# Attention in groups of three quads, and the causal mask of the row maxima added on VectorE

## The chip, the cores and the metric

The kernel runs on one core of a Trainium2 chip. The metric is the device time of one execution in microseconds (us). The median of three runs of the kernel before is 3550.74 us (3547.54 to 3555.72).

## What is computed

One layer of a decoder with two branches, for a prompt of 4096 tokens and for 8 x 4 sampled tokens over a paged cache of 4096 positions. The change lies in the prompt's attention alone: 8 heads of width 64, 4096 queries and keys, float32:

```
s = einsum('bqhd,bkhd->bhqk', q, k) * ATTN_SCALE
s = s + (fq[..., :, None] - fk[..., None, :])      # sums of the log forget gates
s = where(k_pos <= q_pos, s, -inf)
p = softmax(s, axis=-1)
out = einsum('bhqk,bkhd->bqhd', p, v)
```

## The kernel before, in words

The program has five phases, one after another: `phase_project`, `phase_decode`, `phase_attend`, `phase_gates` and `phase_merge`. The change touches `phase_attend` only.

**Blocks and quads.** A block is one head and one tile of 512 queries; there are 64 (8 heads x 8 rows j = 0 to 7). The keys of a block come in quads of 512; row j has j + 1 quads, of which the last is on the diagonal. A head has 36 quads, the kernel 288. A quad is two steps; a step holds the scores of 256 keys by 512 queries, as two halves of 128 keys. `scores(s, half)` issues two matmuls (L1060, L1061) into the PSUM tile `st`, and for a diagonal quad a third, 128 columns wide, that adds the triangular mask (L1064). In diagonal quads the four halves have 512, 384, 256 and 128 columns. ScalarE takes the exponential of a step (L914, or four narrower ones a quad, L918) into `probs`, a ring of RING = 8 steps. GpSimd adds the four parts of a quad's probabilities (L880, L881), and one quad in two of a block to its neighbour (L865), in `quad_sum` with SUMS = 12 slots. `weigh(s)` multiplies the probabilities with v (L1081). `total(b)` takes the denominators of a block with ones (L1093), and `copy_den` on VectorE copies them out.

**Units.** The exponential needs a shift, the maximum of each row, before the block starts. So TensorE computes the scores a second time with queries on the partitions, in units: unit(b, t, c) is 128 queries by 512 keys, one matmul (L1031) into one of two PSUM banks `mx`, and VectorE takes the maximum of the unit (L971, TENSOR_REDUCE). There are 1152 units; 256 are diagonal (c = j), 64 each of 128, 256, 384 and 512 columns. For these TensorE adds the mask with a second matmul, identity by `tri`, 128 columns wide (L1034). The unit after next uses the same bank, and waits until VectorE has reduced it (`bank_free`). `combine(b)` (L978) takes the maximum over the parts of a block, `spread_shift(b)` (L1041, four matmuls) turns it, and ScalarE copies it into `q_one` (L896).

**Order.** TensorE's order is written out by a table. EARLY = 24 units come first, then 144 groups of two quads. A group is: the 8 halves of scores of its four steps, each followed by a unit where the table puts one; the shifts of the blocks that start in the next group (they wait for the exponential of all but the last step of the group, `exp_done`); the four steps of `weigh`; and the totals of blocks that ended one group earlier. A group has 9 units, or 7 if one of its quads is diagonal (after head 0); in a group of 7 no unit stands behind the last half of the diagonal quad. ScalarE waits, from the ninth step on, until the step eight earlier was weighed and its quad summed.

Of the kernel before, what the change touches and what calls it, by code (L numbers as in the profile page):

```python
# [617 lines left out]
def phase_attend(nc, io, keep):  # L618
# [6 lines left out]
    RING = 8  # L625
    SUMS = 12
# [6 lines left out]
    MASKS_READY = 17  # L633
# [15 lines left out]
    NGROUP = NQUAD // 2  # L649
    start_group = [quad_base[b] // 2 for b in range(NB)]  # L650
    end_group = [(quad_base[b + 1] - 1) // 2 for b in range(NB)]
# [10 lines left out]
    def most_units(g):  # L662
        return 7 if g >= quad_base[NT] // 2 and (on_diagonal(2 * g) or on_diagonal(2 * g + 1)) else 9
# [29 lines left out]
    def summed_with_next(n):  # L693

        c = n - quad_base[block_of[n]]
        return c % 2 == 0 and c < row(block_of[n])

# [14 lines left out]
    with ExitStack() as ctx:  # L712
# [7 lines left out]
        tri_raw = m.sb("tri_raw", [P, P])  # L720
        tri_t_raw = m.sb("tri_t_raw", [P, 2 * P])
        tri = m.sb("tri", [P, P], F32R)
# [6 lines left out]
        quad_sum = m.sb("quad_sum", [P, SUMS, TILE])  # L729
# [38 lines left out]
        def _(sp):  # L768
# [57 lines left out]
            for g in range(NGROUP):  # L826
# [7 lines left out]
                b = block_of[2 * g]  # L834
# [16 lines left out]
        def _(pool):  # L851
            nc.gpsimd.memset(tri_raw[:], 0.0)
            nc.gpsimd.memset(tri_t_raw[:], 0.0).then_inc(tri_ready, 1)
            pool.wait_ge(tri_ready, 1)
            nc.gpsimd.affine_select(out=tri_raw[:], in_=tri_raw[:], compare_op=ALU.is_ge, fill=-BIG, base=0,
# [5 lines left out]
            def end(n, last):  # L861

                if n > quad_base[block_of[n]] and summed_with_next(n - 1):
                    chain.link(last)
                    last = nc.gpsimd.tensor_tensor(quad_sum[:, n % SUMS], quad_sum[:, n % SUMS], quad_sum[:, (n - 1) % SUMS], ALU.add)  # L865
                last.then_inc(summed, 1)

            def add_quad(n):

                b = block_of[n]  # L870
                out = quad_sum[:, n % SUMS]
# [20 lines left out]
        def _(act):  # L892
# [42 lines left out]
        def _(dve):  # L935
# [22 lines left out]
            link(nc.vector.tensor_copy(tri[:], tri_raw[:]))  # L958
# [7 lines left out]
            def unit(k):  # L966
# [3 lines left out]
                dve.wait_ge(bank_ready, n + 1)  # L970
                nc.vector.tensor_reduce(max_parts[:, b % AHEAD, t, c:c + 1], mx[:, n % 2, 0:width], AX_X, ALU.max).then_inc(bank_done, 1)  # L971
# [37 lines left out]
        def _(pe):  # L1009
# [9 lines left out]
            def unit(k):  # L1019
                b, t, c = unit_at(k)  # L1020
                h, j = head(b), row(b)
                if k == unit_base[b]:
# [3 lines left out]
                    if j % 2 == 0:  # L1026
# [5 lines left out]
                                        k_one[h % 2][0:KM, c * TILE:c * TILE + width], start=True, stop=(c < j))  # L1032
# [1185 lines left out]
```

## Time and profile before

| | |
|---|---|
| median of three runs | 3550.74 us |
| the profiled execution | 3556.43 us, span 3554.8 us |
| PE busy (matmul) | 3303.2 us, 93% |
| DVE, POOL, ACT busy | 1627.9, 1338.1, 1126.3 us |
| mean granted TensorE clock | 0.96 of 2.4 GHz |

PE is TensorE's matmuls, PEld its weight loads, DVE VectorE, ACT ScalarE, POOL GpSimd. A busy time of PE is the sum of matmul durations, which overlap: the distance from one start to the next is what a matmul costs in the queue. "idle before" is the time in which the engine had nothing before an instruction, with the engine and line that ended it. phase_attend's units, scores and products lie between 1106 and 2545 us of the span.

### The profile page before, as it was taken

The page shows a single profiled execution, that of the slowest core. Times are in us where ns is not written, and L with a number is a line of the kernel's source. Part 1 is how long each engine was busy: PE and PEld are TensorE (multiplying, and loading weights), DVE is VectorE, ACT ScalarE, POOL GpSimd, SP SyncE. Part 2 cuts the span into 40 slices and gives each one's busy share as a digit, 9 for nine tenths or more (in the row PEclk, how much of TensorE's full clock was granted, in tenths as well). Part 3 has the DMA queues.
Part 4 walks back from the last instruction along what each step waited for, and adds up shares of the span by engine and source line. Part 5 has one row for each costly group of instructions (what it writes and reads, how often), then busy time and mean ns, then how long its engine had stood idle before and what let it go on. Part 6 is the DMA issues. An engine that isn't in the chain of part 4 may idle for free. (4 is left out here: it accounts for less than half of the span.)

```text
span 3554.8 us, 49146 instructions
## 1 busy us (share of the span) xinstructions
PE 3303.2 (93%) x17744; PEld 2365.7 (67%) x17744; DVE 1627.9 (46%) x2596; ACT 1126.3 (32%) x1532; POOL 1338.1 (38%) x1273
## 2 busy tenths in 40 slices
PE   8999999696964999999999999999799999959998
PEld 5777777572813666666666666666488888848876
DVE  3333332361615555555555555555343543445554
ACT  4222222141411444444444444454421121111111
POOL 0000000133331787788888888888600000000000
PEclk9999999797985999999999999999899999979999
DMA  5333443599987114141413131410311111055664
GB/s 182 132 125 128 142 158 113 173 365 366 367 312 143 44 37 87 36 89 35 86 37 85 37 85 37 85 33 11 112 72 47 47 68 74 24 183 182 206 206 155
DMA packets 239929, 435.41 MB, mean 122 GB/s; under 512 B 63544, under 2 KB 107577, under 8 KB 237664
## 3 DMA queue, kind: packets, MB, share of 16 engines
q1 hardware_dynamic: 216327, 362.34, 33.5%
q0 software_dynamic: 20768, 68.17, 5.1%
q10 hardware_dynamic: 2656, 2.62, 0.2%
q8 instruction: 101, 1.65, 0.2%
q14 instruction: 77, 0.62, 0.1%
HBM read 314.19 MB, written 119.03 MB: 122 GB/s over the span
## 5 line engine op out<-in xcount | busy, mean ns | idle before, releaser
L971 DVE TENSOR_REDUCE at_max_parts<-at_mx 128x1 f32<-128x512 f32 (+3 forms) x1152 | 737.0, 647 | 410.5 <-PE at_mx L1031 284.6
L914 ACT ACTIVATE at_probs<-at_st,at_gap 128x1024 f32<-128x1024 f32 x448 | 498.6, 1115 | 511.4 <-PE at_st L1061 511.1
L880 POOL TENSOR_TENSOR at_pair_sum<-at_probs 128x1024 f32<-128x1024 f32 x224 | 531.5, 2373 | 196.2 <-ACT at_probs L914 179.7
L1081 PE MATMUL at_o_ps<-at_probs,at_v 128*64 128x512 f32 (+3 forms) x2304 | 499.9, 566 | 0.0
L1031 PE MATMUL at_mx<-at_k_one,at_q_top 71*128 71x512 f32 (+3 forms) x1152 | 461.3, 402 | 14.0 <-DMA at_k_all<-scratch_k_parts 7.9
L1060 PE MATMUL at_st<-at_q_all,at_k_all 128*128 128x512 f32 (+3 forms) x1152 | 459.1, 399 | 6.9 <-ACT at_probs L918 5.6
L1061 PE MATMUL at_st<-at_q_one,at_k_one 67*128 67x512 f32 (+3 forms) x1152 | 440.1, 382 | 0.0
L1081 PEld LDWEIGHTS at_o_ps<-at_probs,at_v 128*64 128x64 f32 x2304 | 171.7, 137 | 246.4 <-issue 184.2
L93 PE MATMUL ga_acc<-ga_h_high,ga_w_high 128*128 128x512 f32 x768 | 299.8, 390 | 0.0
L95 PE MATMUL ga_acc<-ga_h_high,ga_w_low 128*128 128x512 f32 x768 | 299.6, 390 | 0.0
L94 PE MATMUL ga_acc<-ga_h_low,ga_w_high 128*128 128x512 f32 x768 | 299.6, 390 | 0.0
L881 POOL TENSOR_TENSOR at_quad_sum<-at_pair_sum 128x512 f32<-128x512 f32 x224 | 286.2, 1278 | 17.6
L1031 PEld LDWEIGHTS at_mx<-at_k_one,at_q_top 71*128 71x128 f32 x1152 | 221.2, 192 | 97.8 <-issue 41.7
L1060 PEld LDWEIGHTS at_st<-at_q_all,at_k_all 128*128 128x128 f32 x1152 | 220.1, 191 | 77.3 <-issue 43.0
L1061 PEld LDWEIGHTS at_st<-at_q_one,at_k_one 67*128 67x128 f32 x1152 | 220.5, 191 | 36.8
L1597 POOL MEMSET mg_minus_half<- 128x1 f32 x1 | 0.1, 98 | 583.9 <-POOLq L66 583.9
L93 PE MATMUL mg_acc<-mg_w_high,mg_mix_high 128*128 128x512 f32 x512 | 201.1, 393 | 5.2 <-DVE mg_x L1668 5.2
L93 PE MATMUL pj_acc<-pj_h_high,pj_w_high 128*128 128x512 f32 x512 | 202.9, 396 | 1.1 <-DVE pj_kv_rows L459 0.8
L95 PE MATMUL mg_acc<-mg_w_high,mg_mix_low 128*128 128x512 f32 x512 | 200.6, 392 | 0.0
L94 PE MATMUL mg_acc<-mg_w_low,mg_mix_high 128*128 128x512 f32 x512 | 200.3, 391 | 0.0
L296 POOL TENSOR_TENSOR pj_rms<-pj_squares,pj_eps_sum 128x1 f32<-128x1 f32 (+1 forms) x33 | 7.3, 221 | 511.2 <-ACT pj_junk L314 499.3
L95 PE MATMUL pj_acc<-pj_h_high,pj_w_low 128*128 128x512 f32 x512 | 199.6, 390 | 0.0
(318 smaller groups left out, 4957.7 us busy)
## 6 DMA issues: line engine op xcount, KB each, us to landing
dc_pages<-in_cache_k_dram SPq DMA_DIRECT2D x128, 256.0 KB, 5.3
dc_pages<-in_cache_k_dram POOLq DMA_DIRECT2D x128, 256.0 KB, 5.3
dc_pages<-in_cache_v_dram SPq DMA_DIRECT2D x128, 256.0 KB, 8.1
dc_pages<-in_cache_v_dram POOLq DMA_DIRECT2D x128, 256.0 KB, 5.4
scratch_h_t<-pj_h_t SPq DMA_DIRECT2D x8, 2048.0 KB
scratch_q_parts<-pj_stage SPq DMA_DIRECT2D x32, 512.0 KB, 3.4
scratch_k_parts<-pj_stage SPq DMA_DIRECT2D x32, 512.0 KB, 2.8
at_q_all<-scratch_q_parts SPq DMA_DIRECT2D x128, 128.0 KB
```

The costliest lines, as they stand in the source:

```text
L93: nc.tensor.matmul(out, lhs_high, rhs_high, start=first, stop=False)
L94: nc.tensor.matmul(out, lhs_high, rhs_low, start=False, stop=False)
L95: return nc.tensor.matmul(out, lhs_low, rhs_high, start=False, stop=last)
L296: chain.link(nc.gpsimd.tensor_tensor(out, squares[0:rows, n:n + 1], eps_sum[0:rows], ALU.add))
L880: chain.link(nc.gpsimd.tensor_tensor(pair, first, second, ALU.add))
L881: end(n, nc.gpsimd.tensor_tensor(out, pair[:, 0], pair[:, 1], ALU.add))
L914: nc.scalar.activation(probs[:, s % RING], st[:, s % 2], ACT.Exp, bias=bias).then_inc(exp_done, 1)
L971: nc.vector.tensor_reduce(max_parts[:, b % AHEAD, t, c:c + 1], mx[:, n % 2, 0:width], AX_X, ALU.max).then_inc(bank_done, 1)
L1031: last = nc.tensor.matmul(mx[:, n % 2, 0:width], q_top[0:KM, b % AHEAD, t * P:(t + 1) * P], k_one[h % 2][0:KM, c * TILE:c * TILE + width], ...
L1060: nc.tensor.matmul(out, k_all[h % 2][:, keys], q_all[:, b % AHEAD, at:TILE], start=True, stop=False)
L1061: last = nc.tensor.matmul(out, k_one[h % 2][0:KR, keys], q_one[0:KR, b % AHEAD, at:TILE], start=False, stop=(c < j))
L1081: last = nc.tensor.matmul(o_ps[half * HD:(half + 1) * HD, b % 2, at:TILE], v[:, h % 2, 4 * c + own], probs[:, s % RING, half, at:TILE], st ...
```

## The change

- A group has three quads (QUADS = 3, STEPS = 6): 96 groups instead of 144, with 12 halves of scores and then six steps of `weigh`. The ring of probabilities has 12 steps. A group has at most 13 units, or 12 with a diagonal quad after head 0, spread over the twelve places behind the halves; with 12 or fewer none is at the group's start, and with 12 there is one behind the last half of a diagonal quad too. EARLY becomes 29.
- `quad_sum` has 6 slots for the quads that go to `total`, and one for the quads that are added to their neighbour.
- The mask matmul L1034 is gone. For the 256 diagonal units VectorE issues `tensor_tensor_reduce` instead of `tensor_reduce`: it adds `tri` (now float32, 512 wide, zero but for the last 128 columns) to the unit in its PSUM bank, in place, and takes the maximum. It is built as two instructions, both ISA below: the operation, and a second one that writes the 128x1 result and signals.

```diff
-    RING = 8
-    SUMS = 12
+    QUADS = 3
+    STEPS = 2 * QUADS
+    RING = 2 * STEPS
+    SUMS = 6
...
     def most_units(g):
-        return 7 if g >= quad_base[NT] // 2 and (on_diagonal(2 * g) or on_diagonal(2 * g + 1)) else 9
+        return 4 * QUADS if g >= quad_base[NT] // QUADS and any(on_diagonal(QUADS * g + i) for i in range(QUADS)) else 4 * QUADS + 1
...
-        if len(units) > 8:
+        if len(units) > 2 * STEPS:
             return units[place:place + 1]
-        skipped = 8 - len(units)
-        at_end = 4 if on_diagonal(2 * g) else 8
-        places = [p for p in range(1, 9) if p != at_end][:len(units)] if skipped == 1 else list(range(1, 1 + len(units)))
+        places = [1 + i * 2 * STEPS // len(units) for i in range(len(units))]
...
+    def sum_slot(n):
+
+        return SUMS if summed_with_next(n) else kept.index(n) % SUMS
...
@@ GpSimd @@
-                if n >= SUMS:
-                    pool.wait_ge(bank_ready, bank_of["den", block_of[n - SUMS]] + 1)
+                if not summed_with_next(n) and kept.index(n) >= SUMS:
+                    pool.wait_ge(bank_ready, bank_of["den", block_of[kept[kept.index(n) - SUMS]]] + 1)
...
@@ VectorE, unit(k) @@
+                if c == row(b):
+                    nc.vector.tensor_tensor_reduce(out=mx[:, n % 2, 0:width], in0=mx[:, n % 2, 0:width], in1=tri[:, TILE - width:TILE], scale=1.0,
+                                                   scalar=NO_MAX, op0=ALU.add, op1=ALU.max,
+                                                   accum_out=max_parts[:, b % AHEAD, t, c:c + 1]).then_inc(bank_done, 1)
+                    return
                 nc.vector.tensor_reduce(max_parts[:, b % AHEAD, t, c:c + 1], mx[:, n % 2, 0:width], AX_X, ALU.max).then_inc(bank_done, 1)
...
@@ TensorE, unit(k) @@
-                                        k_one[h % 2][0:KM, c * TILE:c * TILE + width], start=True, stop=(c < j))
-                if c == j:
-                    last = nc.tensor.matmul(mx[:, n % 2, t * P:width], ident_r[:], tri[:], start=False, stop=True)
+                                        k_one[h % 2][0:KM, c * TILE:c * TILE + width], start=True, stop=True)
...
@@ TensorE, the groups @@
-                for place in range(8):
-                    scores(4 * g + place // 2, place % 2)
+                for place in range(2 * STEPS):
+                    scores(STEPS * g + place // 2, place % 2)
                     for k in units_after(g, place + 1):
                         unit(k)
                 if starting(g + 1):
-                    pe.wait_ge(exp_done, 4 * g + 3)
+                    pe.wait_ge(exp_done, STEPS * g + STEPS - 1)
                 for b in starting(g + 1):
                     spread_shift(b, starting(g + 1)[0])
-                for s in range(4 * g, 4 * g + 4):
+                for s in range(STEPS * g, STEPS * g + STEPS):
                     weigh(s)
```

TensorE in head 1, row 6, before: the end of a group with a diagonal unit of 256 columns (L1031 and its mask L1034 are the unit, L1060 and L1061 scores, L1081 the product with v, L1093 the total).

```order
L1031 MATMUL at_mx<-at_k_one,at_q_top 128x256
L1034 MATMUL at_mx<-at_tri,at_ident_r 128x128
L1060 MATMUL at_st<-at_q_all,at_k_all 128x512
L1061 MATMUL at_st<-at_q_one,at_k_one 128x512
L1031 MATMUL at_mx<-at_k_one,at_q_top 128x512
L1081 MATMUL at_o_ps<-at_probs,at_v 64x512 x8
L1093 MATMUL at_mx<-at_quad_sum,keep_ones 32x128 x12
```

The same engine in head 1, row 7, in the changed kernel, the end of a group with a diagonal unit of 384 columns (the lines are now L1041 for the unit, L1068, L1069, L1089 and L1101).

```order
L1041 MATMUL at_mx<-at_k_one,at_q_top 128x384
L1068 MATMUL at_st<-at_q_all,at_k_all 128x512
L1069 MATMUL at_st<-at_q_one,at_k_one 128x512
L1041 MATMUL at_mx<-at_k_one,at_q_top 128x512
L1089 MATMUL at_o_ps<-at_probs,at_v 64x512 x12
L1101 MATMUL at_mx<-at_quad_sum,keep_ones 32x128 x16
```

The mask matmul is gone, and twelve products stand together where eight stood. The last places of a group that ends with a diagonal quad, before:

```order
L1031 MATMUL at_mx<-at_k_one,at_q_top 128x384
L1034 MATMUL at_mx<-at_tri,at_ident_r 128x128
L1060 MATMUL at_st<-at_q_all,at_k_all 128x128
L1061 MATMUL at_st<-at_q_one,at_k_one 128x128
L1064 MATMUL at_st<-at_tri_t,at_ident_r 128x128
L1041 MATMUL at_st<-at_ident_r,at_shift_w 65x128 x4
```

And in the changed kernel (L1072 is the mask of the scores, L1049 the shift):

```order
L1041 MATMUL at_mx<-at_k_one,at_q_top 128x512
L1068 MATMUL at_st<-at_q_all,at_k_all 128x128
L1069 MATMUL at_st<-at_q_one,at_k_one 128x128
L1072 MATMUL at_st<-at_tri_t,at_ident_r 128x128
L1041 MATMUL at_mx<-at_k_one,at_q_top 128x512
L1049 MATMUL at_st<-at_ident_r,at_shift_w 65x128 x4
```

A unit now stands between the last half of scores and the shift. VectorE in head 0 of the changed kernel. Before, only `L971 TENSOR_REDUCE` stood here, one a unit, between the small ones that combine and copy:

```order
L977 ISA at_max_parts 128x1
L981 TENSOR_REDUCE at_max_parts<-at_mx 128x1 x2
L977 ISA at_mx,at_max_parts<-at_mx,at_tri 128x256
L977 ISA at_max_parts 128x1
L981 TENSOR_REDUCE at_max_parts<-at_mx 128x1 x2
L977 ISA at_mx,at_max_parts<-at_mx,at_tri 128x384
```

Each diagonal unit is two instructions on VectorE where it was one.

## Rows read from the trace of the kernel before

**Rows 1.** Busy us in a stretch: PE, PEld, DVE, ACT, POOL; clock; DMA share, GB/s.

```profile
1440.00:2500.00 1060.00, 1053.28 (x5878) 681.27 (x5876) 574.28 (x965) 524.99 (x628) 855.51 (x627) 1.00 0.25 54
```

**Rows 2.** Timeline of PE: start us, duration us, instruction; a unit with its mask.

```profile
1519.52 0.40 PE L1031 MATMUL at_mx<-at_k_one,at_q_top 71*128 71x512 f32 x1
1519.76 0.23 PE L1034 MATMUL at_mx<-at_tri,at_ident_r 128*128 128x128 f32 x1
1519.82 0.47 PE L1060 MATMUL at_st<-at_q_all,at_k_all 128*128 128x512 f32 x1
1520.13 0.41 PE L1061 MATMUL at_st<-at_q_one,at_k_one 67*128 67x512 f32 x1
1520.37 0.40 PE L1031 MATMUL at_mx<-at_k_one,at_q_top 71*128 71x512 f32 x1
1520.60 0.40 PE L1060 MATMUL at_st<-at_q_all,at_k_all 128*128 128x512 f32 x1
```

**Rows 3.** Timeline of PE over the end of a group and the next one's start.

```profile
2354.49 0.39 PE L1031 MATMUL at_mx<-at_k_one,at_q_top 71*128 71x512 f32 x1
2354.81 3.65 PE L1081 MATMUL at_o_ps<-at_probs,at_v 128*64 128x512 f32 x16
2358.39 0.50 PE L1060 MATMUL at_st<-at_q_all,at_k_all 128*128 128x512 f32 x1
2358.73 0.39 PE L1061 MATMUL at_st<-at_q_one,at_k_one 67*128 67x512 f32 x1
2358.96 0.22 PE L1031 MATMUL at_mx<-at_k_one,at_q_top 71*128 71x128 f32 x1
...
2359.42 0.40 PE L1061 MATMUL at_st<-at_q_one,at_k_one 67*128 67x512 f32 x1
```

**Rows 4.** Timeline of PE: a diagonal quad at a group's end.

```profile
1511.22 0.22 PE L1064 MATMUL at_st<-at_tri_t,at_ident_r 128*128 128x128 f32 x1
1511.28 0.45 PE L1031 MATMUL at_mx<-at_k_one,at_q_top 71*128 71x512 f32 x1
1511.57 0.28 PE L1060 MATMUL at_st<-at_q_all,at_k_all 128*128 128x256 f32 x1
...
1512.38 0.28 PE L1064 MATMUL at_st<-at_tri_t,at_ident_r 128*128 128x128 f32 x1
1512.70 0.45 PE L1041 MATMUL at_st<-at_ident_r,at_shift_w 128*65 128x128 f32 x4
1513.08 3.22 PE L1081 MATMUL at_o_ps<-at_probs,at_v 128*64 128x512 f32 x16
1516.23 0.43 PE L1093 MATMUL at_mx<-at_quad_sum,keep_ones 128*32 128x128 f32 x8
```

**Rows 5.** Groups by line and shape, DVE: count, busy us, mean ns, idle before.

```profile
L971 DVE TENSOR_REDUCE at_max_parts<-at_mx 128x1 f32<-128x512 f32 x960 | 659.9, 691 | 306.0 <-PE at_mx L1031 284.6 <-PE at_mx L1034 3.1
L971 DVE TENSOR_REDUCE at_max_parts<-at_mx 128x1 f32<-128x128 f32 x64 | 18.6, 290 | 42.7 <-PE at_mx L1034 42.6
L1394 DVE TENSOR_TENSOR ga_stage<-ga_acc,ga_stage 128x512 f32<-128x512 f32 x32 | 22.1, 692 | 155.5 <-ACT ga_stage L1303 150.8 <-DVE ga_pooled L1387 4.3
```

**Rows 6.** Timeline of DVE, a small operation between two others.

```profile
2323.97 0.19 DVE L978 TENSOR_REDUCE at_shift_w<-at_max_parts 128x4 fp32r<-128x32 f32 x1
2324.08 0.28 DVE L971 TENSOR_REDUCE at_max_parts<-at_mx 128x1 f32<-128x128 f32 x1
```

**Rows 7.** Groups by line, ACT: the accumulator read of the projection's squares.

```profile
L314 ACT ACTIVATION_READ_ACCUMULATOR pj_junk<-pj_x 128x1 f32 x28 | 5.2, 187 | 0.0
```

**Rows 8.** Groups by line and shape, POOL.

```profile
L880 POOL TENSOR_TENSOR at_pair_sum<-at_probs 128x1024 f32<-128x1024 f32 x224 | 531.5, 2373 | 196.2 <-ACT at_probs L914 179.7 <-POOL at_quad_sum L865 8.3 <-POOL at_quad_sum L881 7.8
L881 POOL TENSOR_TENSOR at_quad_sum<-at_pair_sum 128x512 f32<-128x512 f32 x224 | 286.2, 1278 | 17.6
```

**Rows 9.** Timeline of DVE among the units ahead of the first group.

```profile
1111.00 1.02 DVE L971 TENSOR_REDUCE at_max_parts<-at_mx 128x1 f32<-128x512 f32 x2 [0.68 <-PE at_mx L1031]
1112.58 1.15 DVE L971 TENSOR_REDUCE at_max_parts<-at_mx 128x1 f32<-128x512 f32 x2 [0.55 <-PE at_mx L1031]
```

More of the change, by code:

```diff
@@ L647, in phase_attend @@
     unit_base = [TT * quad_base[b] for b in range(NB + 1)]
-    NGROUP = NQUAD // 2
-    start_group = [quad_base[b] // 2 for b in range(NB)]
-    end_group = [(quad_base[b + 1] - 1) // 2 for b in range(NB)]
+    NGROUP = NQUAD // QUADS
+    start_group = [quad_base[b] // QUADS for b in range(NB)]
+    end_group = [(quad_base[b + 1] - 1) // QUADS for b in range(NB)]
     def on_diagonal(n):
@@ L696, in summed_with_next @@
         return c % 2 == 0 and c < row(block_of[n])
+    kept = [n for n in range(NQUAD) if not summed_with_next(n)]
+    def sum_slot(n):
+        return SUMS if summed_with_next(n) else kept.index(n) % SUMS
     def dens_after(g):
@@ L719, in phase_attend @@
         q_one = m.sb("q_one", [P, AHEAD, TILE], F32R)
-        tri_raw = m.sb("tri_raw", [P, P])
+        tri = m.sb("tri", [P, TILE])
         tri_t_raw = m.sb("tri_t_raw", [P, 2 * P])
-        tri = m.sb("tri", [P, P], F32R)
         tri_t = m.sb("tri_t", [P, 2 * P], F32R)
@@ L728, in phase_attend @@
         pair_sum = m.sb("pair_sum", [P, 2, TILE])
-        quad_sum = m.sb("quad_sum", [P, SUMS, TILE])
+        quad_sum = m.sb("quad_sum", [P, SUMS + 1, TILE])
         den_out = m.sb("den_out", [P, 2, P])
@@ L851, in _ @@
         def _(pool):
-            nc.gpsimd.memset(tri_raw[:], 0.0)
+            nc.gpsimd.memset(tri[:], 0.0)
             nc.gpsimd.memset(tri_t_raw[:], 0.0).then_inc(tri_ready, 1)
             pool.wait_ge(tri_ready, 1)
-            nc.gpsimd.affine_select(out=tri_raw[:], in_=tri_raw[:], compare_op=ALU.is_ge, fill=-BIG, base=0,
+            nc.gpsimd.affine_select(out=tri[:, TILE - P:TILE], in_=tri[:, TILE - P:TILE], compare_op=ALU.is_ge, fill=-BIG, base=0,
                                     pattern=[[-1, P]], channel_multiplier=1).then_inc(tri_ready, 1)
@@ L864, in end @@
                     chain.link(last)
-                    last = nc.gpsimd.tensor_tensor(quad_sum[:, n % SUMS], quad_sum[:, n % SUMS], quad_sum[:, (n - 1) % SUMS], ALU.add)
+                    last = nc.gpsimd.tensor_tensor(quad_sum[:, sum_slot(n)], quad_sum[:, sum_slot(n)], quad_sum[:, SUMS], ALU.add)
                 last.then_inc(summed, 1)
@@ L870, in add_quad @@
                 b = block_of[n]
-                out = quad_sum[:, n % SUMS]
+                out = quad_sum[:, sum_slot(n)]
                 first, second = probs[:, 2 * n % RING], probs[:, (2 * n + 1) % RING]
                 pool.wait_ge(exp_done, 2 * n + 2)
-                if n >= SUMS:
-                    pool.wait_ge(bank_ready, bank_of["den", block_of[n - SUMS]] + 1)
+                if not summed_with_next(n) and kept.index(n) >= SUMS:
+                    pool.wait_ge(bank_ready, bank_of["den", block_of[kept[kept.index(n) - SUMS]]] + 1)
                 if n + 1 < quad_base[b + 1]:
@@ L1048, in scores @@
                 if half == 0:
-                    if s % 4 == 0 and starting(s // 4):
-                        pe.wait_ge(shift_copied, starting(s // 4)[-1] + 1)
+                    if s % STEPS == 0 and starting(s // STEPS):
+                        pe.wait_ge(shift_copied, starting(s // STEPS)[-1] + 1)
                     if s == first_step[b]:
@@ L1092, in total @@
                     for t in range(TT):
-                        last = nc.tensor.matmul(mx[t * 32:(t + 1) * 32, n % 2, 0:P], keep["ones"][:, 0:32], quad_sum[:, q % SUMS, t * P:(t + 1) * P],
+                        last = nc.tensor.matmul(mx[t * 32:(t + 1) * 32, n % 2, 0:P], keep["ones"][:, 0:32], quad_sum[:, sum_slot(q), t * P:(t + 1) * P],
                                                 start=(q == quads[0]), stop=(q == quads[-1]))
@@ L1108, in _ @@
                 if starting(g + 1):
-                    pe.wait_ge(exp_done, 4 * g + 3)
+                    pe.wait_ge(exp_done, STEPS * g + STEPS - 1)
                 for b in starting(g + 1):
                     spread_shift(b, starting(g + 1)[0])
-                for s in range(4 * g, 4 * g + 4):
+                for s in range(STEPS * g, STEPS * g + STEPS):
                     weigh(s)
```

6 lines of the change are left out of this document (3 added, 3 removed).

## The prediction

> **What bounds the kernel now.** I read four views in this order. First the stretches: in 1060 us in the middle of the attention PE is busy for 1053 us at full clock, while DVE has 574 us, ACT 525 us and POOL 855 us [rows 1]. PE is the limit there, so a change pays only by what it takes out of PE's queue, or costs by what makes PE wait. Second, the timeline of PE, for what an instruction costs in that queue. With 512 columns the start-to-start distance is 0.235 us for scores and units alike: 1520.13 to 1520.60 are two slots [rows 2]. A half of scores with its unit is thus three slots, 0.705 us. Third, the groups of DVE: a unit of 512 columns takes 0.691 us [rows 5], just under PE's 0.705. DVE is idle 306 us before them all the same, since no units come while PE multiplies with v. Fourth, POOL's groups: a full quad costs 2.37 + 1.28 us, and every second one 1.28 us more for the addition to its neighbour, 4.3 us on average [rows 8]. PE needs 4 x 0.705 = 2.82 us for the scores and units of a full quad and 1.72 us for its product (below), 4.54 us. POOL is second.
>
> **1. The mask matmul goes (256 times).** From a masked unit to the second scores matmul behind it is 1519.52 to 1520.13, 0.61 us; without the mask these are two slots, 0.47 us. That is 0.14 us here [rows 2]. For narrow units I have a pair without a mask: a matmul of 128 columns followed by a 512 one, then the next: 1511.22, 1511.28, 1511.57, that is 0.06 + 0.29 = 0.35 us [rows 4]. A masked unit of 128 columns takes 2358.96 to 2359.42 = 0.46 us to the same point [rows 3]. That is 0.11 us, and I take this for all widths: of the two places read it is the lower. A small matmul is too short to cover the next weight load, so the price is twice the 0.06 us that its own columns take. 256 x 0.11 = 28.2 us; in the opening stretch (24 units, 9 of them masked) DVE sets the pace and nothing is won: **-27 us**. Bounds: 256 x 0.06 = 15 us and 256 x 0.14 = 36 us.
>
> The Trainium skill, TensorE: Matmul & The Clock Gate, section "Wait — 56ns, not 53.3ns?", gives a warm 128-column matmul 56 ns from start to start. By that figure alone the term would be an estimated 14 us; rows 2 and 3 both show about double, so the measurement decides.
>
> **2. 96 changes of kind instead of 144.** From the last unit of a group to the first product is 0.32 us instead of 0.235: 0.085 more. Eight products take 3.58 us (the row's 16 are two records each) [rows 3]. A group with a diagonal quad needs 1513.08 to 1516.23 = 3.15 us [rows 4]. Products go in pairs side by side, so that group has 256 columns less, 0.43 us; 512 columns are 0.86 us, four pairs 3.44, and 0.14 us of the 3.58 is paid once a group. The first scores behind it take 0.34 us to the next instead of 0.235, 0.10 more [rows 3]. Together 0.325 us a group; 48 fewer: **-15.6 us**. Bounds: 48 x 0.2 and 48 x 0.33.
>
> **3. Places of the units.** Behind a diagonal quad at the end of a group PE stands from 1512.38 to 1512.70, 0.32 us for a slot of 0.06, until ScalarE has done the last but one step [rows 4]. The change puts a unit there, and also behind a diagonal quad at a group's start, where scores wait for ScalarE. By the table 40 and 24 of the 64 diagonal quads lie so. A slot of up to 0.235 us is then covered by a wait; but in a diagonal quad PE's places are 0.5 to 0.7 us apart and DVE needs 0.69, so most of it goes to waiting for the bank. I take 0.06 each: **-4 us**, between -15 (all of it) and +10 (DVE late by 0.15 us in each).
>
> **4. Opening.** Five more units stand ahead of the first group, where two units take 1.58 us [rows 9]: 5 x 0.79 = 4.0 us, less 5 x 0.235 later, **+2.7 us**. The wider memset of `tri` on POOL is hidden by the load of the keys.
>
> **5. The new instruction on DVE.** Not in the trace. Lower bound: it costs what the reduction does, as adding a PSUM tile and an SBUF tile of 512 columns takes 0.692 us [rows 5]. The second instruction: a small operation of DVE delays the next by 0.11 us [rows 6]; ScalarE's accumulator read is 0.187 us long [rows 7]. I take e = 0.10 us over the reduction, nearest to DVE's own row. What covers it: twelve units of 0.691 are 8.29 us; 2.67 of twelve are diagonal and on average 0.20 us shorter (0.290 at 128 columns, 0.691 at 512 [rows 5]), -0.53; so DVE needs 7.76 + 2.67e = 8.03 us a group. PE wants the bank for the twelfth unit 11 x 0.705 + 0.47 = 8.2 us after the group's start, and needs the tenth reduced by then. DVE starts at 0.9 and has ten at 0.9 + 8.03 x 10/12 = 7.6. There are 0.6 us to spare, 0.3 in a group with a diagonal quad. **0 us**, for any e up to 0.19. Below nothing it cannot be, since PE, busy for 1053 of 1060 us, waits for DVE almost nowhere now [rows 1].
>
> **6. POOL, SP, end.** POOL's 4.3 us plus gaps of about 0.1 us between operations stay under PE's 4.54, and the ring still holds two groups. The slots of `quad_sum` are never needed in the group in which their total is still due (worked through by the table). In the last head the units run out and ScalarE and POOL set the pace for nine quads: **+1 us** of part 2 not won. SP's loads of q still come five groups or more ahead of their units.
>
> **Sum.** -27 - 15.6 - 4 + 2.7 + 1 = -43 us against the profiled execution's 3556.4 us, so 3513. That execution is 5.7 us above the median; against the median the forecast is **3507 us**. Its own range is 3495 to 3522, from the bounds of parts 1 to 3 without all ends meeting.
>
> **Rivals.**
> - *Half rate.* With two float32 tensors DVE takes two cycles a column. The slope of rows 5 is 0.401 us over 384 columns, 1.04 ns a column; 320 columns on average are 0.33 us more, e = 0.43. Ten units are done at 0.9 + 8.91 x 10/12 = 8.3 us: 0.1 us late in 90 groups and 0.3 more in the 56 with a diagonal quad, 25 us: **3532 us**. Against it: the addition at 0.692 us [rows 5]. Chance 0.12. The Trainium skill, Vector Engine (DVE) Microarchitecture Reference, in its list of pitfalls, says that this kind of instruction runs at half throughput with two non-bf16 sources in SBUF; here one source is in PSUM, and no row shows the case.
> - *DVE becomes the bound (slower).* The instruction makes two full passes: 0.49 us more (the mean of the four widths by rows 5) and a read of 0.187, e = 0.68. Ten units at 0.9 + 9.58 x 10/12 = 8.9 us, 0.7 late in 90 groups, +61 us: **3568 us**. It decides from e = 0.58 on, where the lateness, (7.76 + 2.67e) x 10/12 + 0.9 - 8.2, equals the 0.45 us a group that parts 1 to 4 bring. For it: DVE has only 2% to spare against PE's places already. Chance 0.07.
> - *POOL takes over.* Its operations in full quads, gaps included, may reach 4.6 us; then PE's gain in rows 4 to 7 of a head turns into waits of ScalarE for the ring, and only part 1 in the small rows and some of part 2 stay, 25 us: **3526 us**. Against: POOL has 855 of 1060 us [rows 1]. Chance 0.08.
> - *Nothing is won.* The small matmul's slot and the pause at a group's end were only cover for DVE, and PE stands for the bank instead: parts 1 to 3 fall away, **3550 us**. Against: in rows 2 DVE is never what PE waits for. Chance 0.06.
>
> **Numbers.** Forecast 0.67. The range of 3488 to 3542 us takes in the forecast's own, half rate and POOL, reaches 7 us below the forecast's own for part 3 at its best, and leaves out the other two. A measurement of this kernel can tell about 0.2%, 7 us. Faster by more: 0.67 + 0.12 + 0.08 = 0.87, less something for a price that no row shows: 0.85. Same 0.07, slower 0.08.
>
> **What would show it.** The masked stretch must read 0.47 us from unit to second scores. Twelve products must take 3 x 1.72 + 0.14 = 5.3 us. The stretch from the first unit to the last total, 1106 to 2545 us now, must shrink by the whole sum, and the rest of the span by nothing. The new instruction's pair should occupy DVE for 0.8 us at 512 columns, and idle time of PE ended by it should stay under 15 us. A pair of 1.2 us or more with PE idle behind it is half rate; POOL at over 90% of the middle stretch is the third rival. I am wrong above all if the diagonal units cost DVE more than 0.4 us extra.

## The result and the profile after

| | before | changed |
|---|---|---|
| median of four runs each, one chip | 3553.23 us | 3521.20 us |
| lowest to highest | 3547.54 to 3557.71 | 3513.22 to 3525.18 |
| ratio, with its 95% interval | | 0.9908 (0.9884 to 0.9931) |

By the ratio that is 33 us faster, 25 to 41 by the interval. The forecast was 43 us faster against the profiled execution; between the two profiled spans it is 3554.8 - 3519.9 = 34.9 us. The sign and the mechanisms came out as forecast, and the gain is four fifths of the sum.

The head of the changed kernel's page, and the stretch that answers to [rows 1] (busy us of PE, PEld, DVE, ACT and POOL with the number of instructions, then the granted clock, the DMA share and GB/s):

```profile
span 3519.9 us, 48877 instructions
PE 3266.0 (93%) x17488; PEld 2339.1 (66%) x17488; DVE 1632.7 (46%) x2851; ACT 1124.0 (32%) x1532; POOL 1335.7 (38%) x1273
```

```profile
1440.00:2500.00 1060.00, 1054.06 (x5848) 676.91 (x5845) 574.92 (x1149) 538.83 (x647) 885.91 (x647) 1.00 0.24 55
```

PE is as full as before, 1054 of 1060 us, at full clock: what left its queue became time. POOL went from 855 to 886 us because the same work is now done in less time; at 84% it is not the limit.

VectorE's groups by shape, those of [rows 5] and the new instruction (line, engine, operation, shapes and count; busy us and mean ns; idle before):

```profile
L981 DVE TENSOR_REDUCE at_max_parts<-at_mx 128x1 f32<-128x512 f32 x896 | 612.6, 690 | 180.4 <-PE at_mx L1041 166.1
L977 DVE CUSTOM_DVE_ANT_0 at_mx<-at_mx,at_tri 128x512 f32<-128x512 f32 x64 | 44.8, 700 | 32.9 <-PE at_mx L1041 31.9
L977 DVE DVE_READ_ACCUMULATOR2_ANT at_max_parts<- 128x1 f32 x256 | 36.1, 141 | 0.0
L977 DVE CUSTOM_DVE_ANT_0 at_mx<-at_mx,at_tri 128x128 f32<-128x128 f32 x64 | 18.6, 291 | 12.2 <-PE at_mx L1041 12.2
```

The masked maximum has the pace of the reduction, 700 against 690 ns at 512 columns. The second instruction, which reads the accumulator, is 141 ns long. Whether it delays the next unit is read from DVE's timeline in one group (start and length in us), with the unit of TensorE that the last line waits for:

```profile
1527.30 3.39 DVE L981 TENSOR_REDUCE at_max_parts<-at_mx 128x1 f32<-128x512 f32 x5 [0.21 <-PE at_mx L1041]
1530.64 0.57 DVE L977 CUSTOM_DVE_ANT_0 at_mx<-at_mx,at_tri 128x384 f32<-128x384 f32 x1
1531.12 0.14 DVE L977 DVE_READ_ACCUMULATOR2_ANT at_max_parts<- 128x1 f32 x1
1531.35 3.51 DVE L981 TENSOR_REDUCE at_max_parts<-at_mx 128x1 f32<-128x512 f32 x5
...
1530.91 0.40 PE L1041 MATMUL at_mx<-at_k_one,at_q_top 71*128 71x512 f32 x1
```

From the masked unit of 384 columns to the next is 0.71 us, but that is not what the instruction costs: the next unit's matmul runs until 1530.91 + 0.40 = 1531.31, and the reduction starts 0.04 us behind it. In this stretch DVE follows PE's pace. DVE's own pace shows only where the next unit stands ready, and the third experiment has such places: there a masked unit delays the next operation by no more than a plain reduction does. What remains of the second instruction is that it ends later. At 384 columns it ends at 1531.12 + 0.14 = 1531.26, 0.62 us behind the start, where a plain reduction is 0.557 us long (by its group in the third experiment); the bank is given back 0.07 us later.

TensorE at the end of a group with a diagonal quad, which answers to [rows 4]:

```profile
1544.49 0.22 PE L1041 MATMUL at_mx<-at_k_one,at_q_top 71*128 71x128 f32 x1
1544.55 0.45 PE L1068 MATMUL at_st<-at_q_all,at_k_all 128*128 128x512 f32 x1
1544.84 0.39 PE L1069 MATMUL at_st<-at_q_one,at_k_one 67*128 67x512 f32 x1
...
1546.41 0.45 PE L1041 MATMUL at_mx<-at_k_one,at_q_top 71*128 71x512 f32 x1
1546.87 0.28 PE L1072 MATMUL at_st<-at_tri_t,at_ident_r 128*128 128x128 f32 x1
1547.06 0.50 PE L1041 MATMUL at_mx<-at_k_one,at_q_top 71*128 71x512 f32 x1
1547.40 0.41 PE L1049 MATMUL at_st<-at_ident_r,at_shift_w 128*65 128x128 f32 x4
1547.73 4.94 PE L1089 MATMUL at_o_ps<-at_probs,at_v 128*64 128x512 f32 x24
1552.60 0.64 PE L1101 MATMUL at_mx<-at_quad_sum,keep_ones 128*32 128x128 f32 x16
```

The narrow unit without its mask stands 0.35 us ahead of the second scores matmul, as forecast. The last place of the group now has a unit: from the mask of the scores, 1546.87, it is 0.19 us to the unit (the bank) and 0.34 to the shift. The 0.53 us hold a unit where 0.32 us held nothing. The twelve products with a diagonal quad among them take 4.87 us; twelve full ones 5.30 by the same view, as forecast.

### The profile page after: what moved, and what is told of

It is laid out like the page before. It is cut to its first block and busy times, and to the rows that moved or that the text cites. A ratio compares the mean times of both kernels' runs of the same rounds, so it can differ in the third digit from the quotient of the medians.

```text
span 3519.9 us, 48877 instructions
## 1 busy us (share of the span) xinstructions
PE 3266.0 (93%) x17488; PEld 2339.1 (66%) x17488; DVE 1632.7 (46%) x2851; ACT 1124.0 (32%) x1532; POOL 1335.7 (38%) x1273
## 5 line engine op out<-in xcount | busy, mean ns | idle before, releaser
L981 DVE TENSOR_REDUCE at_max_parts<-at_mx 128x1 f32<-128x512 f32 x896 | 612.6, 690 | 180.4 <-PE at_mx L1041 166.1
L1089 PE MATMUL at_o_ps<-at_probs,at_v 128*64 128x512 f32 (+3 forms) x2304 | 490.2, 564 | 0.0
L1041 PE MATMUL at_mx<-at_k_one,at_q_top 71*128 71x512 f32 (+3 forms) x1152 | 466.6, 407 | 18.0 <-DMA at_k_all<-scratch_k_parts 7.8
L1068 PE MATMUL at_st<-at_q_all,at_k_all 128*128 128x512 f32 (+3 forms) x1152 | 449.3, 390 | 4.3 <-ACT at_probs L920 1.6
L1069 PE MATMUL at_st<-at_q_one,at_k_one 67*128 67x512 f32 (+3 forms) x1152 | 440.8, 383 | 0.0
L1089 PEld LDWEIGHTS at_o_ps<-at_probs,at_v 128*64 128x64 f32 x2304 | 179.5, 137 | 261.3 <-issue 219.4
L1041 PEld LDWEIGHTS at_mx<-at_k_one,at_q_top 71*128 71x128 f32 x1152 | 221.4, 192 | 109.5 <-DVE at_max_parts L981 23.6
L1068 PEld LDWEIGHTS at_st<-at_q_all,at_k_all 128*128 128x128 f32 x1152 | 220.4, 191 | 66.5 <-issue 27.4
L1069 PEld LDWEIGHTS at_st<-at_q_one,at_k_one 67*128 67x128 f32 x1152 | 220.7, 192 | 37.1
```

Source lines behind the costliest of these rows:

```text
L1041: last = nc.tensor.matmul(mx[:, n % 2, 0:width], q_top[0:KM, b % AHEAD, t * P:(t + 1) * P], k_one[h % 2][0:KM, c * TILE:c * TILE + width], ...
L1068: nc.tensor.matmul(out, k_all[h % 2][:, keys], q_all[:, b % AHEAD, at:TILE], start=True, stop=False)
L1069: last = nc.tensor.matmul(out, k_one[h % 2][0:KR, keys], q_one[0:KR, b % AHEAD, at:TILE], start=False, stop=(c < j))
L1089: last = nc.tensor.matmul(o_ps[half * HD:(half + 1) * HD, b % 2, at:TILE], v[:, h % 2, 4 * c + own], probs[:, s % RING, half, at:TILE], st ...
```

## The experiments

Each was timed beside the kernel before on its own chip; the medians of that kernel beside them lie between 3553.23 and 3558.24 us, so the ratios and the traces are what can be compared. "Attention" is the time from the start of the first unit to the start of the last matmul of the last total, in the profiled execution; "head" is the distance between the same totals of two heads in the middle of it; "first product" is where `weigh` first issues, counted from the first unit.

| run | median us | ratio (95%) | attention | head | first product |
|---|---|---|---|---|---|
| before | | 1 | 1438.4 | 176.1 | +34.4 |
| changed | 3521.20 | 0.9908 (0.9884 to 0.9931) | 1402.5 | 170.3 | +43.4 |
| groups only | 3540.20 | 0.9956 (0.9942 to 0.9969) | 1420.9 | 172.9 | +43.7 |
| mask only | 3534.63 | 0.9943 (0.9929 to 0.9956) | 1416.8 | 173.1 | +34.1 |
| DVE work twice | 3564.24 | 1.0019 (1.0010 to 1.0028) | 1445.7 | 176.2 | +44.3 |
| small matmuls in the opening | 3517.17 | 0.9888 (0.9873 to 0.9903) | 1397.1 | 170.4 | +38.4 |
| changed, again | 3518.30 | 0.9902 (0.9889 to 0.9915) | 1401.4 | 170.3 | +43.0 |
| small matmuls, again | 3513.38 | 0.9883 (0.9868 to 0.9898) | 1395.7 | 170.4 | +38.7 |
| places from 0 | 3521.69 | 0.9907 (0.9894 to 0.9920) | 1405.0 | 171.0 | +43.1 |
| mask twice (before) | 3579.10 | 1.0072 (1.0057 to 1.0087) | 1462.1 | 179.0 | +36.3 |
| two quads, ring 12 | 3535.97 | 0.9935 (0.9923 to 0.9948) | 1416.2 | 172.8 | +34.4 |
| three quads, ring 8 | 3518.18 | 0.9885 (0.9870 to 0.9899) | 1404.0 | 170.3 | +45.1 |
| small matmuls, v later | 3508.21 | 0.9858 (0.9844 to 0.9873) | 1389.2 | 170.5 | +31.6 |

**One part alone.** The changed kernel with the mask matmul back, and the kernel before with the mask on VectorE. Of each edit the central lines are shown; the making of `tri`, and the lines that the shown ones replace, are left out.

```diff
 TensorE, unit(k), changed kernel
+                if c == j:
+                    last = nc.tensor.matmul(mx[:, n % 2, t * P:width], ident_r[:], tri[:], start=False, stop=True)
```

> Groups of three, the mask still added by TensorE (L1034's matmul kept, VectorE reduces as before). Theory (the parts add up: mask -27, groups and places about -17 us before the opening's cost): 13 to 20 us faster than the kernel before. A middle head (176.1 us before, 170.3 after) at about 173.8. Rival 1 (the mask's slot is only cover for VectorE and all of the gain is the groups'): 30 us faster, the same as the change. Rival 2 (larger groups bring nothing): no change.

```diff
 kernel before: VectorE, unit(k)
+                if c == row(b):
+                    nc.vector.tensor_tensor_reduce(out=mx[:, n % 2, 0:width], in0=mx[:, n % 2, 0:width], in1=tri[:, TILE - width:TILE], scale=1.0,
+                                                   scalar=NO_MAX, op0=ALU.add, op1=ALU.max,
+                                                   accum_out=max_parts[:, b % AHEAD, t, c:c + 1]).then_inc(bank_done, 1)
+                    return
```

> Groups of two as before, mask added by VectorE. Theory: 256 x 0.11 = 27 us faster less what VectorE's second instruction makes PE wait, 20 to 27 us; a middle head at about 172.6. Rival 1 (the slot was cover): PE waits for the bank instead, less than 7 us faster, with PE idle behind the new instruction. If e1 and e2 add up to more than the change's own 32 to 36 us, the parts stand in each other's way.

The groups alone bring 16 us by the ratio (17.5 of attention), the mask alone 20 (21.6). Their sum, 39 us in the traces, is near the 36 of both together. Per head the groups save 3.2 us and the mask 3.0; together 5.8. The forecast, without its opening and end, was 46.6 / 8 = 5.8 us a head. But eight heads at 3.2 us would be 26 us for the groups, and the trace has 17.5. The rest is lost outside the middle heads: the first product stands at +43.7 instead of +34.4.

The parts do stand in each other's way a little: 3.2 + 3.0 a head is 0.4 us more than 5.8, so behind the groups the mask brings 172.9 - 170.3 = 2.6. PE's idle time ahead of the units that DVE's maxima end is 8.4 us in all before, 10.2 with the groups alone, 22.5 with the mask alone and 30.7 in the changed kernel. Most of it comes with the mask on VectorE; the groups alone add next to none.

**How near DVE is to being the bound.** One more reduction of the same bank ahead of each masked one, its result unused.

```diff
+                    nc.vector.tensor_reduce(spare[:, b * TT + t:b * TT + t + 1], mx[:, n % 2, 0:width], AX_X, ALU.max)
                     nc.vector.tensor_tensor_reduce(
```

> The changed kernel with one more reduction of the same unit ahead of each diagonal unit's instruction, so the diagonal unit costs VectorE 0.49 us more on average (0.29 to 0.69), e = about 0.6 in all. My sum gave a break-even at e = 0.58: the time should come back to that of the kernel before, within 10 us. Rival (the two banks and the products absorb more than I counted): under 15 us slower than the changed kernel. Other rival (VectorE already sets the pace): the full 256 x 0.49 = 125 us slower than the changed kernel.

DVE in this kernel where both units stand ready (L978 is the spare reduction, L979 the masked maximum and its read), the middle stretch, and PE's idle time ahead of all units that L979 ends:

```profile
1803.73 0.56 DVE L978 TENSOR_REDUCE at_spare<-at_mx 128x1 f32<-128x384 f32 x1 [5.74 <-PE at_mx L1043]
1804.21 0.56 DVE L979 CUSTOM_DVE_ANT_0 at_mx<-at_mx,at_tri 128x384 f32<-128x384 f32 x1
1804.68 0.14 DVE L979 DVE_READ_ACCUMULATOR2_ANT at_max_parts<- 128x1 f32 x1
1804.68 0.69 DVE L978 TENSOR_REDUCE at_spare<-at_mx 128x1 f32<-128x512 f32 x1
1805.28 0.69 DVE L979 CUSTOM_DVE_ANT_0 at_mx<-at_mx,at_tri 128x512 f32<-128x512 f32 x1
1805.89 0.14 DVE L979 DVE_READ_ACCUMULATOR2_ANT at_max_parts<- 128x1 f32 x1
1805.89 0.69 DVE L983 TENSOR_REDUCE at_max_parts<-at_mx 128x1 f32<-128x512 f32 x1
```

```profile
1440.00:2500.00 1060.00, 1043.03 (x5681) 655.78 (x5679) 640.54 (x1349) 523.20 (x628) 854.88 (x627) 1.00 0.24 54
...
  DVE at_max_parts L979: 88.1, 208
```

The distance from one start to the next is 0.47 or 0.48 us at 384 columns and 0.60 or 0.61 at 512, whether the operation is the plain reduction or the masked one, and the read starts together with the next operation. So at these widths the price of the masked maximum in DVE's queue is e = 0.0, and the spare reduction adds 0.61, 0.48, 0.33 and 0.20 us at 512, 384, 256 and 128 columns, 0.41 on average.

The whole gain is gone and 7 us more: the changed kernel's attention grows by 43 us. The crossing lies below 0.41, where the prediction put it at 0.58. Its own sum gave the half-rate rival, at e = 0.43, only 25 us. PE's busy time falls from 1054 to 1043 of 1060 us, though DVE is busy for only 641: PE stands ahead of a unit for 88.1 / 208 = 0.42 us at a time until a masked unit's bank is free, 208 times for 256 of them. Not all of these 88 us are lost, but the lateness is paid at each masked unit and does not average over ten. That the time came back near that of the kernel before, as expected, is partly luck: the added work was smaller than reckoned, and the cover was thinner.

**The opening.** Two small full-float32 matmuls behind each of the 29 first units, into a part of `st` that is written later anyway.

```diff
             for k in range(EARLY):
                 unit(k)
+                for i in range(2):
+                    nc.tensor.matmul(st[:, 1, 1, 0:P], keep["ones"][:], keep["ident"][:], start=True, stop=True)
```

> The changed kernel with two more matmuls of 128 columns in full float32 (ones by identity, result unused) behind each of the 29 opening units, where TensorE stands idle between units. It tests whether the clock, 0.50 until about 48 us after the first unit in the changed kernel and until about 37 us in the kernel before, is what the opening loses. Theory: PE busy in the opening brings the clock to 1.00 before the first group, and the first group runs in half the time: 6 to 12 us faster than the changed kernel. Rival (the clock rises only with the products and the extra work just delays the units): no change or up to 10 us slower.

The ratio, 0.9888, lies inside the interval of the changed kernel's first comparison, so both were run again, side by side.

> The changed kernel itself, unaltered, as the yardstick for the three runs beside it on the same chip. Both theories: 32 to 36 us faster than the kernel before.

> The kernel of e4 once more, now beside e5. In e4's trace the units ran from 1106.3 to 2451.5 us, 7 us less than in the changed kernel. Theory (the clock in the opening is worth what that trace shows): 5 to 9 us faster than e5. Rival (the gain is noise of other phases): within 3 us of e5.

Side by side it is 3518.30 against 3513.38, 4.9 us, just under the expected 5 to 9, and 5.7 us of attention. The two intervals, 0.9889 to 0.9915 and 0.9868 to 0.9898, overlap, so the traces carry this verdict. Stretches of 10 us (busy us of PE, PEld, DVE, ACT and POOL; the number behind POOL is the clock), first of the changed kernel:

```profile
1124.00:1134.00 10.00, 9.32 (x23) 5.09 (x23) 6.59 (x15) 1.07 (x2) 0.00 (x0) 0.50 1.10 216
1134.00:1144.00 10.00, 10.00 (x29) 8.26 (x29) 5.32 (x11) 4.22 (x6) 3.22 (x5) 0.50 1.15 213
1144.00:1154.00 10.00, 10.00 (x39) 6.43 (x39) 2.86 (x6) 3.08 (x6) 6.54 (x7) 0.58 0.96 212
1154.00:1164.00 10.00, 10.00 (x52) 7.69 (x52) 8.04 (x16) 7.43 (x10) 5.17 (x3) 1.00 0.47 122
```

With the small matmuls, second run (this execution began the attention 1.1 us earlier). The first three stretches are cut where the clock changed:

```profile
1103.22:1109.50 6.28, 6.28 (x27) 6.09 (x28) 3.08 (x10) 0.00 (x0) 0.00 (x0) 0.50 1.32 225
1109.50:1116.30 6.80, 4.52 (x35) 4.17 (x34) 4.29 (x12) 0.00 (x0) 0.00 (x0) 1.00 1.05 221
1116.30:1123.20 6.90, 6.11 (x24) 5.73 (x25) 2.80 (x6) 0.00 (x0) 0.00 (x0) 0.51 1.05 220
1123.00:1133.00 10.00, 9.31 (x74) 8.65 (x73) 8.82 (x19) 1.07 (x2) 0.00 (x0) 0.99 1.10 213
```

And before:

```profile
1126.00:1136.00 10.00, 9.72 (x34) 7.64 (x34) 5.33 (x10) 3.07 (x6) 0.82 (x2) 0.50 1.13 210
1136.00:1146.00 10.00, 10.00 (x36) 6.20 (x35) 2.93 (x5) 3.42 (x4) 5.24 (x5) 0.63 1.13 208
1146.00:1156.00 10.00, 10.00 (x58) 6.81 (x57) 6.64 (x13) 4.72 (x7) 6.74 (x7) 1.00 1.04 243
```

Taking each mean as a step from 0.50 to 1.00, the clock rises at 1143.4 before (0.63 over 1136 to 1146), 37 us behind the first unit, and in the changed kernel at 1152.4, 48 us behind it. This is 3 and 5 us behind the first product. The changed kernel's first group is longer, and all of its scores are paid at half clock. With the small matmuls the clock rises twice: 6 us behind the first unit, down again at 1116.3 while PE stands 3.07 us for the queries of a unit (until 1117.09, shown below), and for good at 1123.2, 20 us behind the first unit and before the first scores. From the first scores to the first product it is then 9.1 us where the changed kernel has 15.6.

Cut at the start of the last product of head 0 and of head 6, attention falls into three parts, all in us:

| | head 0 | heads 1 to 6 | head 7 to the last total |
|---|---|---|---|
| before | 204.8 | 1056.6 | 177.0 |
| changed | 206.7 | 1021.8 | 173.9 |
| changed, again | 205.7 | 1021.9 | 173.8 |
| with the small matmuls (second run) | 199.8 | 1022.0 | 173.9 |

The six heads fall by 34.8 us and head 7 by 3.1. Head 0 does not fall at all: it is 1.9 us longer, 0.9 in the second run. The small matmuls take 5.9 us out of head 0, beside the changed kernel again, and nothing elsewhere.

**The places.** The list starts at place 0, so that the last place of a group of twelve units is empty again, as before the change.

```diff
-        places = [1 + i * 2 * STEPS // len(units) for i in range(len(units))]
+        places = [i * 2 * STEPS // len(units) for i in range(len(units))]
```

> The changed kernel with the units of a group of twelve or fewer one place earlier: the first stands ahead of the group's scores, and none behind the last half, so also none behind a diagonal quad that ends a group. Theory (part 3 of the prediction: a unit there fills the wait for ScalarE): 3 to 12 us slower than e5, with 0.32 us from the last scores matmul to the shift again. Rival (the unit there only moves the wait to VectorE's bank): within 3 us of e5, or faster.

It costs 3.4 us against the changed kernel run beside it (3.6 of attention, about 0.6 in each middle head), the size of part 3; the two intervals overlap, so again the trace decides. The shift's own idle time, first with places from 0, then in the changed kernel:

```profile
L1049 PE MATMUL at_st<-at_ident_r,at_shift_w x256: 219/224/314, 1131.5 to 2462.6; 128*65 128x128 f32 x128
...
  ACT at_probs L924: 10.3, 41
```

```profile
L1049 PE MATMUL at_st<-at_ident_r,at_shift_w x256: 218/223/314, 1130.3 to 2458.2; 128*65 128x128 f32 x128
...
  ACT at_probs L920: 1.6, 1
  DVE at_shift_w L988: 1.2, 1
```

The pause for ScalarE ahead of the shift, 10.3 us in 41 places, is gone in the changed kernel.

**The price of one mask matmul.** In the kernel before it is issued twice (the second adds the mask to what is masked already, so the maxima are the same).

```diff
                 if c == j:
+                    nc.tensor.matmul(mx[:, n % 2, t * P:width], ident_r[:], tri[:], start=False, stop=False)
                     last = nc.tensor.matmul(mx[:, n % 2, t * P:width], ident_r[:], tri[:], start=False, stop=True)
```

> The kernel before with the mask matmul issued twice for every diagonal unit (the same 128 columns added again, result unchanged since both entries are hugely negative). It prices the matmul alone, with nothing else moved. By 0.11 us each: 27 us slower than the kernel before. A second narrow matmul behind a narrow one could cost only its 0.06 us (with the next weights already held up once): 15 us slower is the low end. Rival (the slot is cover for VectorE): under 7 us slower.

Attention grows by 23.7 us: 23.7 / 256 = 0.093 us each (25.6 us by the ratio, 0.10). PE's queue around a pair of them:

```profile
1522.31 0.40 PE L1031 MATMUL at_mx<-at_k_one,at_q_top 71*128 71x512 f32 x1
1522.55 0.23 PE L1034 MATMUL at_mx<-at_tri,at_ident_r 128*128 128x128 f32 x1
1522.61 0.27 PE L1035 MATMUL at_mx<-at_tri,at_ident_r 128*128 128x128 f32 x1
1522.72 0.45 PE L1061 MATMUL at_st<-at_q_all,at_k_all 128*128 128x512 f32 x1
1523.01 0.39 PE L1062 MATMUL at_st<-at_q_one,at_k_one 67*128 67x512 f32 x1
```

The second mask starts 0.06 us behind the first, its columns' time, but that distance is not the price, since the matmuls behind are held up too. From the unit to the second scores matmul it is 1522.31 to 1523.01, 0.70 us, where [rows 2] have 0.61 with one mask and 0.47 without. Compared unit by unit in the kernel before and in the one with the mask alone (the 240 masked units behind the opening), the same distance is longer by 0.110 to 0.115 us in the median at each of the four widths, and by 0.107 on average; the 18 with products behind them have 0.06 to 0.07. These are 25.7 us of queue in all, of which 21.6 come off attention.

**Group or ring.** The change also made the ring of probabilities longer. These two tell which of the two it needs: groups of two with 12 steps of ring, groups of three with 8.

```diff
-    QUADS = 3
+    QUADS = 2
     STEPS = 2 * QUADS
-    RING = 2 * STEPS
+    RING = 12
```

> The changed kernel with groups of two again (QUADS = 2), but with its own ring of 12 steps, its sum slots, its rule for the places of the units, and the mask on VectorE. Theory (the gain of the groups is the number of changes between scores and products, not the longer ring): about the time of e2, 19 to 24 us faster than the kernel before, a middle head near 173.1 us. Rival (the ring lets ScalarE run ahead of GpSimd, and that is the gain): 30 us or more faster, a middle head near 170.3. Second rival (the rule for places matters): groups with a diagonal quad now take 8 units instead of 7, so VectorE is asked for more there; slower than e2 by 5 us or more.

```diff
-    RING = 2 * STEPS
+    RING = 8
```

> The changed kernel, groups of three, with the ring of 8 steps of the kernel before. ScalarE may then be only four quads ahead of GpSimd, and the sixth step of a group waits for the quad before the group's first. Theory (number of changes): up to 8 us slower than the changed kernel, the loss visible as idle time of ScalarE ended by GpSimd's quad_sum. Rival (the ring is the gain): all of the 16 us that e1 brought are lost, 15 to 25 us slower.

With groups of two and the longer ring attention takes 1416.2 us, the mask alone 1416.8. With groups of three and the short ring it is 1404.0 against 1402.5, and the run's median is the changed kernel's within the noise. ScalarE's idle time that GpSimd would end does not appear: TensorE's scores end 391 of its 392 us ahead of the wide exponentials. The ring contributes nothing that can be measured; the gain is that of the longer group.

**A version that beats both.** The small matmuls, and the 1024 KB load of v put behind the third load of keys instead of the first, so that the opening's q arrives earlier.

```diff
-                if c == 0:
+                if c == 2:
                     load_v(0)
```

> The kernel of e4 and e6 with the load of v for head 0 issued after the third piece of k and the query blocks 1 to 3 instead of after the first. In the changed kernel the opening's units wait 4.7 us for a block of q behind that load, which alone holds SP's queue for 5 us. Theory: the first product comes 3 to 5 us earlier, unless v is late for it; 37 to 46 us faster than the kernel before. Rival (the 16 DMA engines are full in the opening, so the order of issue moves nothing, or v is late): no better than e6, 41.6 us.

3508.21 us, 0.9858 (0.9844 to 0.9873): 50 us under the kernel before, more than the expected 37 to 46, and its interval lies below that of the changed kernel run again, 0.9889 to 0.9915. TensorE's only long pause in the opening was for the queries of a unit, here in the changed kernel, and behind it the kernel with the small matmuls alone:

```profile
1117.56 1.22 PE L1041 MATMUL at_mx<-at_k_one,at_q_top 71*128 71x512 f32 x2 [4.70 <-DMA at_q_one<-scratch_q_parts]
```

```profile
1117.09 0.80 PE L1041 MATMUL at_mx<-at_k_one,at_q_top 71*128 71x512 f32 x1 [3.07 <-DMA at_q_one<-scratch_q_parts]
```

In this last version no unit waits for queries; the first scores stand 22.5 us behind the first unit, where it was 29.6 with the small matmuls alone. The load of v was what stood in SP's queue ahead of the queries. But only 3.1 of these 7.1 us are the pause itself. Without the pause the clock rose 3.5 us behind the first unit and did not fall again:

```profile
1102.88:1106.40 3.52, 3.52 (x16) 3.52 (x17) 1.47 (x6) 0.00 (x0) 0.00 (x0) 0.50 1.09 228
1106.40:1125.38 18.98, 18.29 (x140) 17.04 (x139) 16.70 (x40) 1.07 (x2) 0.00 (x0) 1.00 1.13 218
```

By subtraction the other 4 us go with the clock; no run changes the clock alone. The later load of v without the small matmuls was not run, so what it is worth alone is not shown.

## Why the prediction was right, and where a term was off

- **The mechanism** was right: PE bound the middle of the attention, and each head shrank by what left its queue. Forecast 5.8 us a head, measured 5.8 (176.1 to 170.3). That the two agree to a tenth is luck: the groups gave 0.7 us a head more than forecast, and the mask behind them 0.8 less.
- **Part 1, the mask matmul** (-27, "0.11 us, and I take this for all widths"): the price was right, 0.107 us on average and a median of 0.11 at each width. Too high was the share of it that comes off. The mask alone brings 21.6 us of attention, inside the stated 15 to 36, and behind the groups 2.6 us a head where part 1 made 27 / 8 = 3.4. The likely reason is PE's waiting for VectorE's maxima, which grows in the two kernels with the mask on VectorE (8.4 us to 22.5 and 30.7); no run takes these waits away. The mask matmul issued twice costs 23.7 us, 0.093 each. The Trainium skill's 56 ns (TensorE: Matmul & The Clock Gate, section "Wait — 56ns, not 53.3ns?") agrees with the distance from the first mask to the second, 0.06 us, but as the price of a mask it would make 14 us, and the runs show 22 to 24.
- **Part 2, changes of kind** (-15.6): 12 products took 5.30 us, as forecast. With part 3 inside, the groups gave 3.2 us a head where parts 2 and 3 made (15.6 + 4) / 8 = 2.45. Too low by 0.7 us; no run shows where they come from.
- **Part 3, places** (-4): 3.4 to 3.6 us by its own run. As written there, the bank takes back part of it: 0.53 us at the group's end for 0.32 before.
- **Part 4, opening** (+2.7): this is the term that failed. Ahead of the first scores the five units cost 27.8 - 23.4 = 4.4 us, as forecast (4.0). Left out was that the first group itself is longer by four places and that everything up to the first products runs at half clock. From the first scores to the first product it is 15.6 us instead of 11.0. Of the whole 9.0 us, 1.2 for five units and 4 x 0.705 = 2.8 for four places are work that comes off later; 5.0 stay, and the rise of the clock nearly 2 us later behind the first product adds about one more. By the table of the three parts head 0 was to fall by 5.8 - 2.7 = 3.1 us and rose by 1.9: 5.0 of the 7 us between the forecast's -43 and the trace's -36. The opening explains 6 - 2.7 = 3.3 of these 5.0; the rest is not located, and 1 us of it is the difference between two runs of the changed kernel. With the clock up early head 0 falls by 5.0. Of the other 2 us most lies in head 7 and the end (-3.1 where -4.8 was forecast).
- **Part 5, DVE** (0 us at e = 0.10): 0 was nearly right, on two wrong sizes that happen to offset. The sum priced PE by the distance from start to start but DVE by the length of its operations, 0.691 us a unit; where the next unit stands ready the distance is 0.61, so DVE had more room than the 2% stated. And e is 0.0 in DVE's queue, with the bank given back 0.07 us later. On the other side the test of the tenth unit is too kind: the third experiment cost 43 us at 0.41. The sign for it was badly chosen too. PE's idle time ended by the new instruction was to stay under 15 us and is 4.3. But the waits end mostly with a plain reduction: 26.4 us against 8.4 before. 3 us of them lie in the opening. The rest are about 0.2 us each, in 11 places of one middle head.
- **Part 6, POOL**: 886 of 1060 us, below the 90% named. The end is unchanged: the last total waits for `at_quad_sum` in both kernels.
- **Rivals.** Half rate needed e = 0.43 and a pair of 1.2 us or more: refuted by 700 + 141 ns. The Trainium skill's rule (Vector Engine (DVE) Microarchitecture Reference, section "Points that are easy to get wrong") is about two sources in SBUF; here one source is in PSUM, and no run tested it. DVE as the bound: refuted for this instruction, confirmed as a mechanism by the third experiment, at 0.41 us more a masked unit. POOL: refuted by its 84%. Nothing won: refuted by both halves of the change, though about 4 of the mask's 25.7 us of queue did not come off.

PE's rows that answer to this point, before and after (the engine's idle time ahead of the units, us and times, by what ended it; the first line is before, the others after, where L977 is the new instruction):

```profile
  DVE at_max_parts L971: 8.4, 19
```

```profile
  DVE at_max_parts L981: 26.4, 104
  DVE at_max_parts L977: 4.3, 14
  issue: 22.3, 38
```

## What to carry to other kernels

A small matmul between large ones costs more of the queue than its columns, here 0.11 us for 0.06, so moving 256 of them to an engine that has a pass over the same data anyway pays, as long as that engine's lateness, worked out for each buffer that it gives back, stays under the slack. At 54% busy VectorE had little of it: 0.41 us more a masked unit took all of the gain and 7 us more. Price every engine by the distance from one start to the next, and only where its next input stands ready: a length overstates the cost (0.69 for 0.61 us), and a distance beside a slower engine is that engine's. When a steady loop is made longer, price its first turn separately: it runs at the clock and with the loads of the opening. Here that took up to 5 us of a forecast 43, and mending the opening (clock and order of loads; the kernel before waits 4.03 us for the same queries) was worth 12 to 13 us of attention. The ring that was made longer with it should be tested alone; here it did nothing.

## What the runs showed of the hardware

- The clock did not follow TensorE's busy share. Over 1124 to 1134 us in the changed kernel PE is busy 9.32 of 10 us at 0.50; over 1123 to 1133 us with the small matmuls 9.31 at 0.99. Over 1134 to 1144 us the changed kernel's PE was busy 10.00 of 10 us, with scores and units, at 0.50, and the clock rose only after the first products with v had begun, here and in the kernel before. With two small full-float32 matmuls behind each unit it rose 6.3 us behind the first unit, fell during a pause of 3.07 us and rose again; without the pause it rose after 3.5 us and stayed. Whether the kind of the added matmuls or their number did it, the runs don't tell apart.
- VectorE's masked maximum over a PSUM tile and an SBUF tile, both float32, has the pace of the plain reduction: 700 against 690 ns long at 512 columns, and 0.61 us to the next operation where that stands ready. The read of the accumulator is 141 ns long and runs beside the next operation; it costs no distance (0.47 us at 384 columns, plain 0.48), but the result comes 0.07 us later.
- A mask matmul of 128 columns costs 0.11 us of TensorE's queue where matmuls of 512 columns follow, and 0.06 to 0.07 where products follow (the kernel before against the one with the mask alone).
